# Order of the softmax and eviction steps in the attention layers of a chained two-block kernel: remainders put into pauses, softmax bias per sub-tile, key projection in other PSUM banks

## The reference

```python
def dense_attend(q, k, v, scale):                       # layers 0 and 3
    s = jnp.einsum('bqhd,bkhd->bhqk', q, k).astype(jnp.float32) * scale
    p = jax.nn.softmax(s, axis=-1).astype(v.dtype)
    return jnp.einsum('bhqk,bkhd->bqhd', p, v)
...
def sink_attend(scores, values, sink_l):                # layer 1
    sink_col = jnp.broadcast_to(sink_l[None, :, :, None, None], scores[0].shape[:-1] + (1,))
    p = jax.nn.softmax(jnp.concatenate(scores + [sink_col], axis=-1), axis=-1)
...
q_x, k_x = apply_rope_2(q_x, ...), apply_rope_2(k_x, ...)   # rotation, on the 512 tokens only
y = (o * jax.nn.silu(gate)) @ w_out
```

## Time and profile before

| | |
|---|---|
| median of 3 runs | 3189.52 us (3187.19 to 3190.22) |
| profiled execution, its own time | 3177.51 us |
| its span | 3175.7 us |
| busy: PE, DVE, ACT | 2901.7 us, 1843.6 us, 1150.1 us |
| the chain that ended last, by engine | PE 78%, DVE 13%, ACT 6% |
| attention of layer 0, from 1215 us to 1447 us | PE busy 217.69 of 232 us |
| attention of layer 1, from 1635 us to 1998 us | PE busy 287.16 of 363 us |
| attention of layer 3, from 2940 us to 3110 us | PE busy 165.44 of 170 us |

### The profile page before, as it was taken

One profiled execution on the slowest core, in us unless ns is written; L12 is line 12 of the kernel. 1 busy time (PEld: TensorE's weight loads), 2 busy tenths in 40 slices (PEclk: granted clock), 3 DMA queues, 4 the chain that ended last, 5 costly groups with the idle time before them and its releaser, 6 DMA issues.

```text
span 3175.7 us, 35948 instructions
## 1 busy us (share of the span) xinstructions
PE 2901.7 (91%) x14361; PEld 2328.8 (73%) x14361; DVE 1843.6 (58%) x3265; ACT 1150.1 (36%) x2022; POOL 93.9 (3%) x177
## 2 busy tenths in 40 slices
PE   7999879999999997999988778999998887989997
PEld 5767648778888886888877666778875556767886
DVE  6446678877675567543645546464535666455444
ACT  4234242232223433444534434443322110454443
POOL 0000000100000000000100000020000000000000
PEclk9999989999999999999999999999998998999999
DMA  6222115645453232002210110332321211321102
GB/s 233 100 87 87 62 51 206 223 165 181 154 186 103 103 120 90 27 17 103 91 46 21 30 30 4 113 117 100 117 74 51 63 43 34 116 83 57 40 17 93
DMA packets 109312, 288.77 MB, mean 91 GB/s; under 512 B 18326, under 2 KB 37815, under 8 KB 108888
## 3 DMA queue, kind: packets, MB, share of 16 engines
q1 hardware_dynamic: 97880, 249.05, 23.7%
q0 software_dynamic: 9392, 32.48, 2.8%
q10 hardware_dynamic: 1872, 4.93, 0.4%
HBM read 257.05 MB, written 24.12 MB: 89 GB/s over the span
## 4 chain that ended last, share of the span: by engine, by line
PE 78%; DVE 13%; ACT 6%; issue 1%; DMA 0%; ACTq 0%; SPq 0%; POOL 0%; DVEq 0%; POOLq 0%
PE ps L1801 19%; PE ps L1803 19%; PE ps L1802 19%; PE ps L2036 4%; PE ps L2094 2%; PE ps L2068 2%; PE ps L1834 2%; PE ps L2023 2%; PE ps L2110 1%; ACT pt L2366 1%; ACT tmp L2358 1%; PE ps L1950 1%; PE ps L2057 1%; DVE tmp L2888 1%; DVE tmp L2702 1%
## 5 line engine op out<-in xcount | busy, mean ns | idle before, releaser
L1801 PE MATMUL ps<-hh,whi 128*128 128x256 f32 (+1 forms) x2424 | 919.3, 379 | 47.6 <-DVE q L2894 23.1
L1803 PE MATMUL ps<-hh,wlo 128*128 128x256 f32 (+1 forms) x2424 | 871.4, 359 | 0.0
L1802 PE MATMUL ps<-hl,whi 128*128 128x256 f32 (+1 forms) x2424 | 871.3, 359 | 0.0
L1801 PEld LDWEIGHTS ps<-hh,whi 128*128 128x128 f32 x2424 | 460.0, 190 | 155.0 <-issue 50.0
L1802 PEld LDWEIGHTS ps<-hl,whi 128*128 128x128 f32 x2424 | 461.1, 190 | 90.2 <-issue 21.4
L1803 PEld LDWEIGHTS ps<-hh,wlo 128*128 128x128 f32 x2424 | 459.1, 189 | 71.4
L2551 DVE TENSOR_TENSOR wlo<-raw,whi 128x1024 fp32r<-128x1024 f32 x249 | 304.0, 1222 | 233.8 <-ACT whi L2173 233.3
L2173 ACT ACTIVATE whi<-raw 128x1024 fp32r<-128x1024 f32 x249 | 262.5, 1055 | 294.4 <-PE ps L1803 278.3
L2036 PE MATMUL ps<-pt,v 128*128 128x256 f32 x768 | 210.2, 396 | 28.2 <-ACT pt L2366 16.1
L2366 ACT ACTIVATE pt<-ps 128x512 f32<-128x512 f32 (+1 forms) x200 | 109.6, 578 | 244.5 <-PE ps L2023 244.3
L2862 DVE TENSOR_REDUCE sm<-ps 128x1 f32<-128x768 f32 (+3 forms) x176 | 124.7, 735 | 93.2 <-PE ps L1993 47.4
(11 more groups left out here) (373 smaller groups left out, 4543.0 us busy)
## 6 DMA issues: line engine op xcount, KB each, us to landing
raw<-in_wall SPq DMA_DIRECT2D x249, 512.0 KB, 4.2
mb<-in_wmod SPq DMA_DIRECT2D x128, 512.0 KB, 3.5
xb<-xpark SPq DMA_DIRECT2D x24, 384.0 KB, 4.6
xpark<-F POOLq DMA_DIRECT2D x32, 256.0 KB, 2.4
upark<-tmp POOLq DMA_DIRECT2D x18, 384.0 KB, 2.8
u<-upark SPq DMA_DIRECT2D x24, 256.0 KB, 2.9
tmp<-tmp SPq DMA_DIRECT2D x80, 64.0 KB, 2.0
early<-in_wm SPq DMA_DIRECT2D x8, 512.0 KB, 6.9
```

The costliest lines, as they stand in the source:

```text
L1801: e.matmul(out, L[0], R[0], start=start, stop=False)
L1802: e.matmul(out, L[0], R[1], start=False, stop=False)
L1803: return e.matmul(out, L[1], R[0], start=False, stop=stop)
```

## The change

Five edits, all in the order of the work. The matmuls are the same and in the same order.

1. Remainders come in three parts (rotation, high, low) and are due in *gaps*. A push has two: the first behind the scores and the bias of u, where DVE later waits for the exponentials, the second at its end. `later(f, n)` counts gaps, not pushes.
2. The modulation sums move into the first gap of a push that has no remainder there (`pumps=0` at the projections of the attention loops).
3. The bias is made per sub-tile: maximum, bias, maximum, bias. In layer 1 the small exponential of the sink goes ahead of the second large one, and waits for the sink part of the bias.
4. The key projection of layer 1 uses the two transpose banks.
5. The transposes of a chunk go sub-tile by sub-tile, so the first ones need only the first sub-tile's normalisation.

Remainders made before the first unit are kept and played by `att.begin()` (in layer 0 behind the first value projection, in layer 1 behind the first query projection).

```diff
@@ rope_stages
-        def halves():
+        def high():
             stage("rope_split", m, c_ - a_, hi, lo, name, free)
+
+        def low():
+            stage("rope_split_lo", m, c_ - a_, hi, lo, name)
             tmps.drop(m)
-        later(turn)
-        later(halves, 1)
+        for n, f in enumerate((turn, high, low)):
+            later(f, n)
@@ class Attend
             if self.before is None:
-                f()
+                self.first.append(f)
...
+        def gap(self):
+            fs = self.rests.popleft() if self.rests else ()
+            for f in fs:
+                f()
+            return fs
...
                 stage("score", u, s, u["bk"][s], u["sm"])
-            stage("bias", u, u["sm"])
+                stage("bias", u, s, u["sm"])
...
         def push(self, u):
-            b, rests = self.before, self.rests.popleft() if self.rests else ()
+            b = self.before
             self.before = u
             n = (len(b["keys"]) + 1) // 2 if b else 0
             if u:
                 self.scores(u)
+            if not self.gap():
+                pump()
             self.multiply()
...
                 self.normalise(u)
-            for f in rests:
-                f()
+            self.gap()
@@ stacked (queries; high and low as above), context part
             if context:
-                context(stack)
+                context(high, 1)
+                context(low, 2)
@@ make_k, make_q of layer 1
-            play(tile_stages(KD, H, tH, SEGS, evac, at=att.spare()[0:2]))
+            play(tile_stages(KD, H, tH, SEGS, evac, at=att.spare()[1:][::-1], pumps=0))
...
-                    later = att.later if n % 2 == 0 else lambda f, n=0: att.later(f)
+                    later = lambda f, i, last=1 + n % 2: att.later(f, min(i, 3 - last))
...
-            play(tile_stages(KD, H, tH, SEGS, evac, at=att.spare()[0:2]))
+            play(tile_stages(KD, H, tH, SEGS, evac, at=att.spare()[0:2], pumps=0))
@@ PE, turn
-            for q in range(n):
-                for s in range(2):
-                    w.wait_ge(*dve.of(("prob", u["l"], u["h"], u["qt"], s)))
+            for s in range(2):
+                w.wait_ge(*dve.of(("prob", u["l"], u["h"], u["qt"], s)))
+                for q in range(n):
@@ ACT, exp
-            wait_all(w, (dve, ("mx", l, h, qt)), t)
             S_ = SM[:, sm.i, :]
+            if u["kind"] == "swa" and s:
+                w.wait_ge(*dve.of(("sk", l, h, qt)))
+                A(S_[:, 6:8], S_[:, 6:8], ACT.Exp).then_inc(*act.up(("es", l, h, qt)))
+            wait_all(w, (dve, ("mx", l, h, qt, s)), t)
@@ DVE, bias
-            w.wait_ge(*dve.of(("mx0", l, h, qt, 1)))
+            w.wait_ge(*dve.of(("mx0", l, h, qt, s)))
             if u["kind"] == "mla":
-                TS(S_[:, 2:4], S_[:, 0:2], -u["scale"], None, ALU.mult).then_inc(*dve.up(("mx", l, h, qt)))
+                TS(S_[:, 2 + s:3 + s], S_[:, s:s + 1], -u["scale"], None, ALU.mult).then_inc(*dve.up(("mx", l, h, qt, s)))
...
```

More of the change, by code:

```diff
@@ L1169, in __init__ @@
             self.ptr, self.before, self.chunk, self.nt, self.n = ptr, None, None, 0, 0
-            self.rests, self.side = deque(), [0, 0]
+            self.rests, self.first, self.side = deque(), [], [0, 0]
         def spare(self):
@@ L1185, in later, with begin @@
                 self.rests[n].append(f)
+        def begin(self):
+            for f in self.first:
+                f()
+            self.first = []
+        def gap(self):
+            fs = self.rests.popleft() if self.rests else ()
+            for f in fs:
+                f()
+            return fs
         def scores(self, u):
@@ L1272, in turn, with high, low @@
                 tmps.drop(j)
-            def stack():
-                stage("stack", None, None, TMP[:, m.i, 0:NX], m, dst[:, :, a:b], name, free)
+            def high():
+                stage("stack", None, TMP[:, m.i, 0:NX], dst[:, :, a:b], name, free)
+            def low():
+                stage("stack_lo", TMP[:, m.i, 0:NX], dst[:, :, a:b], name, m)
                 tmps.drop(m)
-            later(turn)
-            later(stack, 1)
-        else:
-            def stack():
-                stage("stack", g, bank, ps[:, bank.i, 0:b - a], None, dst[:, :, a:b], name, free)
+            for n, f in enumerate((turn, high, low)):
+                later(f, n)
+        else:
+            def high():
+                stage("stack", g, ps[:, bank.i, 0:b - a], dst[:, :, a:b], name, free)
+            def low():
+                stage("stack_lo", ps[:, bank.i, 0:b - a], dst[:, :, a:b], name, bank)
                 banks.drop(bank)
             if context:
-                context(stack)
-            else:
-                stack()
+                context(high, 1)
+                context(low, 2)
+            else:
+                high()
+                low()
     def mla(l, j, enter, with_ctx, att_free):
@@ L1372, in evac @@
                     banks.drop(g.banks[i])
[L1373 removed]
+            play(tile_stages(2, CKP, tk, None, evac, tok=6, at=att.spare(), pumps=0))
         def make_qr(pair):
@@ L1380, in evac @@
                     stacked(g, i, QR[:, q.i, :, :], ("qr" if a == NC_ else "qrc", l, pair), (q, free), att.later)
-            play(tile_stages(4, CQP, tq, gr, evac, warm=() if pair else [(None, 9)], at=att.spare()[2 - len(gr):2]))
+            play(tile_stages(4, CQP, tq, gr, evac, warm=() if pair else [(None, 9)], at=att.spare()[2 - len(gr):2], pumps=0))
         def make_qk(h):
@@ L1427, in mla @@
         make_v(0)
+        att.begin()
         for _ in make_qk(0):
@@ L2359, in exp @@
             x.then_inc(*act.up(("ex", l, h, qt, s), *bk))
-            if u["kind"] == "swa" and s:
-                w.wait_ge(*dve.of(("sk", l, h, qt)))
-                A(S_[:, 6:8], S_[:, 6:8], ACT.Exp).then_inc(*act.up(("es", l, h, qt)))
         def turn(u, c, n, b, p):
@@ L2366, in turn, with stack @@
             A(PT[:, p.i, 0:256 * n], ps[:, b.i, 0:256 * n], ACT.Copy).then_inc(*act.up(("pt", u["l"], u["h"], u["qt"], c), b))
-        def stack(g, b, src, m, dst, name, free):
+        def stack(g, src, dst, name, free):
             wait_all(w, (pe, g) if g else (dve, ("roped", name)), free)
@@ L2568, in rope_add, with rope_split_lo @@
             TT(tm, tm, rot, ALU.add).then_inc(*dve.up(("roped", name), j))
-        def rope_split(m, n, hi, lo, name, free):
+        def rope_split_lo(m, n, hi, lo, name):
             w.wait_ge(*act.of(name))
@@ L2872, in bias @@
                 w.wait_ge(*dve.of("nsink"))
-                STT(S_[:, 2:4], S_[:, 0:2], -u["scale"], sink, ALU.mult, ALU.min).then_inc(*dve.up(("mx", l, h, qt)))
-                w.wait_ge(*dve.of(("mx", l, h, qt)))
-                TT(S_[:, 6:8], S_[:, 2:4], sink, ALU.subtract).then_inc(*dve.up(("sk", l, h, qt)))
+                STT(S_[:, 2 + s:3 + s], S_[:, s:s + 1], -u["scale"], sink[:, s:s + 1], ALU.mult, ALU.min).then_inc(*dve.up(("mx", l, h, qt, s)))
+                if s:
+                    w.wait_ge(*dve.of(("mx", l, h, qt, 1)))
+                    TT(S_[:, 6:8], S_[:, 2:4], sink, ALU.subtract).then_inc(*dve.up(("sk", l, h, qt)))
         def weights_of(u, sm, t):
@@ L2889, in weights_of, with stack_lo @@
                 x.then_inc(*dve.up(("prob", l, h, qt, s), *([sm] if s else [])))
-        def stack(g, b, src, m, dst, name, free):
+        def stack_lo(src, dst, name, b):
             w.wait_ge(*act.of(name))
@@ L2894, in stack @@
                 x = TT(dst[64:128, s, :], src[64 * s:64 * s + 64, :], dst[0:64, s, :].bitcast(F32), ALU.subtract)
-            x.then_inc(*dve.up(name, b if g else m))
+            x.then_inc(*dve.up(name, b))
         def take(u):
@@ L3017, in vector_program @@
               "coef_in": coef_in, "coef_out": coef_out, "o_split": o_split, "out_square": out_square, "out_add": out_add, "rope_raw": rope_raw,
-              "latent": latent, "silu": silu, "half": half, "score": score, "bias": bias, "weights_of": weights_of, "stack": stack, "take": take,
+              "latent": latent, "silu": silu, "half": half, "score": score, "bias": bias, "weights_of": weights_of, "stack_lo": stack_lo, "take": take,
               "sine": sine, "conv3": conv3, "filter": filter_, "kf": kf, "fw_in": fw_in, "fold": fold,
```

9 lines of the change are left out of this document (4 added, 5 removed).

## The result

The changed kernel takes 3139.98 us (median of 4 runs, 3137.42 to 3140.77), the kernel before, run beside it, 3189.87 us (3187.19 to 3192.23): a ratio of 0.9848, with an interval of 0.9836 to 0.9859, 49.9 us less. The prediction was 3142.4 us. Its total held; two of its terms were wrong by 12 and by 7 us in opposite directions, and that is what the experiments are about.

A forecast was written before the change was run, and what follows sets the result against it. The prediction took PE, busy 91% of the span, as the bound, so its idle or slow time counted, mostly in layer 1's attention. Terms of 27.0 + 4.8 + 3.3 + 4.2 + 0.8 + 6 + 1 = 47.1 us gave 3142.4 us, range 3130 to 3162.

The forecast's parts named there:

- Part 1: Layer 1's key projections, tiles 0, 2, 4: waits of 23.1 us vanish, 3.9 us more from the clock; 27.0 us won.
- Part 2: Layer 1, tiles 0, 2, 4, behind the key projection: moving the key rotation into the pause, with split bias, wins 4.8 us.
- Part 3: Layer 1's units: split bias starts the first exponential 0.6 us earlier; 0.8 us saved per tile, booked within other parts.
- Part 4: Layer 1's odd tiles 1, 3, 5: rotations leave the path, context low part comes later; 3.3 us won net.
- Part 5: Layer 1's tiles 6 and 7: rotation and copies leave tile 6's path; 4.2 us won there, 0.8 us in tile 7.
- Part 6: Layer 0: modulation sums no longer stand ahead of evictions, so PE's waits for low parts shrink; 6 us won.
- Part 7: Layer 1's transposes go by sub-tile, so the first sub-tile's no longer wait behind the second's; 1 us won.
- A: Rival, chance 0.17: DVE's pauses are too short and added small operations cost 15 us; gain only 26 us, 3163 us.
- B: Rival, chance 0.12: shorter waits end slow-clock stretches in layer 1; 11 us more won, 3131 us.
- C: Rival, chance 0.04: layer 1's stretches from qt 5 to the next query projection fall to half clock; 17 us slower, 3206 us.
- D: Rival, chance 0.03: the key projection waits again, at transposes for the key's context part, and remainders cancel out; 3185 us.

The follow-up runs named there:

- key_back: The changed kernel with layer 1's key projection back in the first transpose bank and the output bank: 3159.3 us.
- after: The changed kernel itself, all five edits made to the kernel before: 3139.98 us, ratio 0.9848.
- mods_back: The changed kernel with the modulation sums of layers 0 and 3 ahead of the evictions again, remainders left in the pauses: 3148.3 us.
- bias_joined: The changed kernel with one bias operation for both sub-tiles again and the small sink exponential behind the second large one: 3140.2 us.
- ctx_first: The changed kernel with the queries' context part evicted ahead of the rotated part in odd tiles: 3125.0 us, run again 3124.6 us.
- key_as_before: ctx_first with the three steps of a key's remainders where the kernel before had them: 3118.2 us.
- mods_only: The kernel before with only the modulation sums of layers 0 and 3 moved behind a unit's biases: 3180.9 us.

## Why the prediction was right, and which of its terms were not

- **Part 1 (27.0 us): right, also in its size.** 24.1 us ahead of the projections and 3.9 us in them; alone 26.6. What the working didn't say is that parts 1 and 2 share the wait (key_back: 18 us).
- **Part 2 (+4.8 us): wrong, and the largest error.** The stretch became 2.2 us longer in each of three tiles, -6.8 us. Two steps failed. The first is "such a copy and its swap together took 3.0 us, so the rotation can start at about 1679.5". 3.0 us is the copy and the activity of the DMA (0.62 + 2.41 us); the instruction that waits for it starts 1.42 us later still. The timeline couldn't show this, since DVE came late there. Two rows of the same trace could, where DVE was waiting:
```profile
1610.13 0.59 ACT L2194 ACTIVATE tmp<-ps 128x512 f32<-128x512 f32 x1
...
1610.75 2.48 SPq L3163 DMA_DIRECT2D tmp<-tmp  x4
...
1614.66 0.69 DVE L2564 TENSOR_TENSOR tmp<-tmp,cs 128x512 f32<-128x512 f32 x1 [3.97 <-DMA tmp<-tmp]
```
  From copy to rotation 4.53 us. The Trainium skill, DMA: Bandwidth & Descriptors, Anatomy of one DMA, says that the semaphore of a DMA can't fire until the last byte is confirmed landed; it describes the other issuing path, but the 1.42 us here, from row to row, agree in kind. With these 4.5 us the rotation starts at 1680.9 in the prediction's frame and the normalisation 2.3 us late instead of 0.85: the 2.0 us won ahead of the maxima are gone, and PE is caught by a longer wait. This turns the gain into nothing: the idle time of the three stretches fell by 0.6 us in all. The second step is that the sum put PE's clock in this stretch at nothing: the busy time rose by 7.4 us. The sizes hold for these two executions. With the key's remainders in their old place the stretch takes 22.8 to 25.2 us, 23.6 in the mean of twelve (four traces); in the new place 23.7 to 26.7 us, 25.1 in the mean of eighteen (after, key_back, mods_back, bias_joined and the two of ctx_first), so that 1.5 us each are nearer than 2.2. key_as_before, which moves only this, has 22.4 us three times.
- **Part 3 (6.4 us in eight tiles): right in direction, 3.7 us by the stage, 4.9 by its idle time.** The scores' wait went to 1.36 us, not 1.2. The rule of the Trainium skill (VectorE: DVE Perf Modes, Rules for kernel authors) on the count of DVE operations did not decide here: the 48 of them in layer 1 stand where DVE had 79.6 us of pauses, and without them the stage is longer.
- **Part 4 (3.3 us): 2.4 us** (3.5 of idle time), with the value wait at 3.21 us, as "nearly 3 us". That it could be halved by an exchange of two neighbours (ctx_first) the working had in hand and passed over.
- **Part 5 (5.0 us): 5.3 us**; tile 6's wait is 1.43 us, 1.2 forecast.
- **Part 6 (6 us): 12.9 us.** The waits of the earlier trace rows went (7.1 us), but not by the step that the term gives as the reason: with the sums back ahead of the evictions they are still down to 2.3 us (mods_back), and with the sums alone moved 4.4 us are left (mods_only). It is the remainders' new places that took most of them. And the term left out the first unit, whose projection waited 9.5 us for the low part of the keys, outside the stretch of the earlier trace rows that I read; it waits 4.3 us now.
- **Part 7 (1 us)** was not tried alone.
- **The total.** By its terms 47.1 us, and layer 1 at about 322 us, where it takes 334.0; the two profiled executions differ by 40.1, with 5.2 us against the changed kernel from the start of the program, so 45.3. The medians differ by 49.9, since the kernel before runs at a lower clock as a rule than in its profiled execution. A term that is 11.6 us off in part 2 and 7 us missing in part 6 met by chance, as did 3.3 us that the trace shows outside the two stages (1.0 lost between them, 4.3 won behind layer 1, of which 1.1 are the first wait of layer 3, 4.50 us before and 3.41 now) and that no part speaks of; the total is better than its working.
- **The rivals.** A is out by bias_joined. B's mechanism exists, but the change itself didn't bring it (0.94 in layer 1); only key_as_before ended the stretches at half clock in layer 1, but for one at 1911 us: 276.6 us busy against 289.2. C and D did not happen.

## What to carry to other kernels

Before an operation is moved up behind a transfer, take the time from the transfer's source to its consumer from a place where the consumer was waiting; a place where it came late shows only when the transfer was over. In an engine's queue of remainders, put first what another engine waits for, and look at every queue that a moved step passes: each of the three failures here was one neighbour too early. Split a stage's time into PE's idle and busy time before you explain it: here 2.5 us of clock stood behind what looked like a longer wait, and in ctx_first 3.2 us less idle time in the odd tiles came with 3.3 us less busy time. And take a second trace of the kernel before.

## What the runs showed of the chip that was not expected

**Nearly the same idle time, another clock.** Layer 1's idle time is 44.8 us in the changed kernel and 41.0 in key_as_before, but the busy time of the same matmuls falls from 289.2 to 276.6 us. In the changed kernel PE runs at 0.50 right behind the 2.7 us wait of tile 0; in key_as_before, where no wait for the normalisation is over 1.3 us, the stage has 0.99. That the longest waits decide this is a guess that fits these two; it is not shown. The two traces of the kernel before have the same waits, up to 7.7 us, and differ by 8.6 us of busy time (0.95 and 0.92). What does repeat is the mean granted clock over the whole span: 0.969 or 0.970 in four timed runs of the changed kernel, 0.975 to 0.979 in five of key_as_before.
```profile
1668.50:1671.00 2.50, 2.47 (x10) 2.04 (x11) 2.21 (x7) 1.06 (x2) 0.00 (x0) 0.50 0.00 0
```
**The start differs between executions, and the clock column doesn't show it.** In the first 50 us the same groups of matmuls take twice as long at first and then their usual time, and the moment of the change differs from execution to execution. Before, then after:
```profile
17.77 2.93 PE L1834 MATMUL ps<-tmp,ones 128*128 128x512 f32 x4
...
22.25 1.54 PE L1834 MATMUL ps<-tmp,ones 128*128 128x512 f32 x4
```
```profile
29.54 2.91 PE L1859 MATMUL ps<-tmp,ones 128*128 128x512 f32 x4
...
34.24 1.54 PE L1859 MATMUL ps<-tmp,ones 128*128 128x512 f32 x4
```
The profile's column gives a granted clock of 1.00 in both. That is no reading: the traces hold no record of the clock before 20.6 us and 32.8 us, the moments at which the durations change, and the column counts what has no record as full speed. By the durations PE is at half clock from its first matmul (14.1 and 13.9 us) to there. This makes the first wait for the weights' low part end at 51.2 us in one trace and at 56.8 in the other, before anything that the change touches; in other traces it is 51.4 to 60.2. Stages are therefore better compared from a mark of their own than by spans.
